# V projected over high and low halves and transposed, VectorE's masks ahead of its decays, halved level sums, one-comparison picks, and the last norm ahead of the branch

## The reference, cut to what matters

```
x    = LN(x)
proj = x @ w_in                       # q, f, v, output gate: 8 heads x 128 each; conv pair; two gates
logf, k = functions of f              # forget gate and key
per head, blocks of 64 tokens:        # gated linear recurrence, 128x128 state S
   b    = cumsum(logf)
   attn[t,s] = sum_d q[t,d] k[s,d] exp(b[t,d] - b[s,d])   for s <= t
   o    = attn @ v + (q exp(b)) @ S ;   S = exp(b_last) S + (k exp(b_last - b))^T @ v
A    = rms_norm(o) * silu(g) @ w_o_a
B    = conv module (31 taps, LayerNorm, silu) @ w_o_b
x    = LN(alpha x + (sig(gate_a) A + sig(gate_b) B) @ w_out)
router: 16 experts, best of 4 groups, then top 2 in it
x    = LN(alpha x + sum_e gate_e * (silu(x Wg_e) * (x Wu_e)) Wd_e)
```

## Time and profile before

| | us |
|---|---|
| median of 3 runs | 913.27 (912.89 to 913.73) |
| the profiled execution | 911.96 |
| its span | 910.1 |
| TensorE busy | 848.2 (93%) |
| VectorE busy | 397.4 (44%) |
| ScalarE busy | 227.5 (25%) |
| GpSimd busy | 108.1 (12%) |
| mean granted TensorE clock | 0.989 |

### The profile page before, as it was taken

One profiled execution on the slowest core, in us unless ns is written; L12 is line 12 of the kernel. 1 busy time (PEld: TensorE's weight loads), 2 busy tenths in 40 slices (PEclk: granted clock), 3 DMA queues, 4 the chain that ended last, 5 costly groups with the idle time before them and its releaser, 6 DMA issues.

```text
span 910.1 us, 12810 instructions
## 1 busy us (share of the span) xinstructions
PE 848.2 (93%) x4904; PEld 532.4 (58%) x4904; DVE 397.4 (44%) x720; ACT 227.5 (25%) x358; POOL 108.1 (12%) x173
## 2 busy tenths in 40 slices
PE   4999999999999999999999999999999899898983
PEld 3989888898989866546554353535435244252330
DVE  6787788879999823215310313103031040310205
ACT  6566666653356131003010011000100001000001
POOL 1366667620000000000000000000000000000000
PEclk9999999999999999998999999999999999999997
DMA  8222222524436523905499999999999999999951
GB/s 302 71 79 80 78 78 85 188 80 154 171 104 237 212 107 153 372 0 208 163 429 428 428 428 428 426 428 427 429 427 429 428 428 428 428 428 428 427 255 59
DMA packets 30420, 248.95 MB, mean 274 GB/s; under 512 B 4462, under 2 KB 7918, under 8 KB 17962
## 3 DMA queue, kind: packets, MB, share of 16 engines
q1 hardware_dynamic: 27840, 247.07, 66.2%
q10 hardware_dynamic: 2538, 1.32, 0.5%
HBM read 245.89 MB, written 2.48 MB: 273 GB/s over the span
## 4 chain that ended last, share of the span: by engine, by line
PE 53%; DVE 19%; DMA 15%; POOL 5%; issue 4%; ACT 3%; POOLq 0%; DVEq 0%; ACTq 0%; SPq 0%
PE ps L437 52%; DMA ring<-in_w_up_e 8%; DMA ring<-in_w_gate_e 7%; DVE ar L1503 6%; DVE split_t L1511 3%; POOL ring L1240 2%; DVE ring L1390 1%; DVE ring L1403 1%; POOL ring L1226 1%; PE ps L772 1%; DVE split_w L1349 1%; POOL ar L1255 0%; DVE mid L1521 0%; POOL ar L1253 0%; DVE split_w L1354 0%
## 5 line engine op out<-in xcount | busy, mean ns | idle before, releaser
L437 PE MATMUL ps<-ring,ar 128*64 128x512 f32 (+1 forms) x1120 | 268.2, 594 | 10.6 <-DMA ring<-in_w_gate_e 3.9
L437 PEld LDWEIGHTS ps<-ring,ar 128*64 128x64 f32 (+1 forms) x1120 | 99.1, 140 | 168.5 <-issue 152.6
L437 PE MATMUL ps<-ring,xT 128*64 128x512 f32 (+2 forms) x896 | 161.4, 458 | 7.0 <-DMA ring<-in_w_gate_e 6.7
L437 PEld LDWEIGHTS ps<-ring,xT 128*64 128x64 f32 (+1 forms) x896 | 84.3, 152 | 79.0 <-issue 63.8
L1720 DVE TENSOR_TENSOR ar<-ar,ps 128x512 f32<-128x512 f32 (+1 forms) x42 | 28.7, 684 | 224.4 <-PE ps L437 224.4
L437 PE MATMUL ps<-split_x,split_t 128*128 128x320 f32 x672 | 101.7, 313 | 4.7 <-DVE split_t L1511 4.1
L437 PEld LDWEIGHTS ps<-split_x,split_t 128*128 128x128 f32 x672 | 100.1, 191 | 6.0 <-issue 3.8
L437 PE MATMUL ps<-split_x,split_w 128*128 128x320 f32 x480 | 80.4, 324 | 6.6 <-DVE split_w L1354 2.7
L437 PEld LDWEIGHTS ps<-split_x,split_w 128*128 128x128 f32 x480 | 73.8, 195 | 11.1 <-issue 2.5
L437 PE MATMUL ps<-ar 128*64 128x64 f32 (+6 forms) x304 | 74.1, 375 | 3.1 <-ACT ar L1174 1.2
L1503 DVE SCALAR_TENSOR_TENSOR ar<-ar,params 128x350 f32<-128x350 f32 x116 | 67.7, 584 | 4.1
(11 more groups left out here) (190 smaller groups left out, 721.8 us busy)
## 6 DMA issues: line engine op xcount, KB each, us to landing
ring<-in_w_gate_e SPq DMA_DIRECT2D x32, 2048.0 KB, 27.5
ring<-in_w_up_e SPq DMA_DIRECT2D x32, 2048.0 KB, 25.9
ring<-in_w_down_e SPq DMA_DIRECT2D x32, 2048.0 KB, 31.7
ring<-in_w_in SPq DMA_DIRECT2D x56, 512.0 KB, 4.3
ring<-in_w_o_a SPq DMA_DIRECT2D x8, 512.0 KB, 5.9
ring<-in_w_out SPq DMA_DIRECT2D x1, 4096.0 KB, 14.6
ring<-in_w_o_b SPq DMA_DIRECT2D x4, 512.0 KB, 5.1
ar<-in_x_prompt SPq DMA_DIRECT2D x2, 512.0 KB, 4.5
```

The source lines that it names most:

```text
L437: return pe.matmul(out, lhsT, rhs, start=start, stop=stop)
```

## The change

Five groups of edits.

1. V goes through `project` as F and Q do, with features on the partitions. ScalarE makes a third high piece (`w_high(..., 2)`), VectorE a third low piece (`w_low(..., 2)`). ScalarE copies the product out of PSUM into a new buffer `hvT` (`v_features`), TensorE transposes it in three pieces (`v_tokens`, behind `prev_out`), and ScalarE's `v_copy` takes it from there.
2. VectorE does both masks before `level_decay`, and a new addition `level_fold` (three banks of 192 columns) takes over GpSimd's two first additions. GpSimd is left with three. The copy into `hebl` moves from VectorE to ScalarE.
3. The position table holds slot + 1, zero where a token isn't chosen. A pair's picks are one copy and one comparison over 384 columns, its gate picks one multiplication.
4. x1's first tile is transposed before the last mix tile; two `keep_busy` calls before the logits go, eight become six and two become one. `gather` signals each half, and `gate` waits for the second half only at its third group.
5. The last norm is applied tile by tile between the statistics, ahead of the branch; in the branch it would be done again.

```diff
+            def v_tokens(i, b):
+                pe.wait_ge(h["vT_sb"], 2 * i + b + 1)
+                for t, (t0, n) in enumerate(TILES):
+                    last = pe.transpose(ps[0:n, 3, t * P:t * P + P], hvT[:, t0:t0 + n], ident)
+                last.then_inc(h["vt_done"], 1)
...
             def cur_v(i, b, first):
-                value_tile(b, 0)
-                value_tile(b, 1)
-                value_tile(b, 2).then_inc(h["v_done"], 1)
+                n = 2 * i + b
+                pe.wait_ge(wlo_ready, 3 * n + 3)
+                if not first:
+                    pe.wait_ge(h["v_sb"], n)
+                project(3, piece(wh, 2), piece(wl, 2)).then_inc(h["v_done"], 1)
...
                 cur_v(*cur, first)
                 if prev:
                     prev_out(*prev, first_prev)
+                v_tokens(*cur)
```

ScalarE, in `head_turn` and in what it calls:

```diff
+            def v_features(i, b):
+                n = 2 * i + b
+                act.wait_ge(h["v_done"], n + 1)
+                signal(act, act.activation(hvT, ps[:, 3, 0:T], ACT.Copy), h["vT_sb"], n + 1)
...
             def v_copy(i, b, first):
-                act.wait_ge(h["v_done"], n + 1)
+                act.wait_ge(h["vt_done"], n + 1)
...
                 cc(act.activation(heb, hb, ACT.Exp))
+                cc(act.activation(hebl[:, b, :], heb[:, SEQ - 1:T:DEC], ACT.Copy))
...
                     u_high(1)
                 elif not first:
                     w_high(*nxt, 1)
+                v_features(*cur)
+                if nxt:
+                    w_high(*nxt, 2)
                 v_copy(*cur, first)
```

VectorE and GpSimd:

```diff
+            def level_fold(i, b):
+                n = 2 * i + b
+                signal(dve, dve.tensor_tensor(hAM[:, :, 0:3 * BLK], hAM[:, :, 0:3 * BLK], hAM[:, :, 4 * BLK:LW], ALU.add), h["fold_ready"], n + 1)
...
                 forget_in(*cur, first or first_prev)
-                level_decay(*cur)
                 if prev:
                     level_mask(*prev, first_prev)
                     last_mask(*prev, first_prev)
+                    level_fold(*prev)
+                level_decay(*cur)
...
                 carry_side(*cur, first)
+                if nxt:
+                    w_low(*nxt, 2)
...
-                pc(pool.tensor_tensor(am[:, :, 0:3 * BLK], am[:, :, 0:3 * BLK], am[:, :, 4 * BLK:LW], ALU.add))
...
+                pool.wait_ge(h["fold_ready"], n + 1)
+                pc(pool.tensor_tensor(hAM[:, :, 0:2 * BLK], hAM[:, :, 0:2 * BLK], hAM[:, :, 2 * BLK:4 * BLK], ALU.add))
+                signal(pool, pool.tensor_tensor(hAS[BLK:P, 0:2, BLK:P], hAM[BLK:P, 0:2, 0:BLK], hAM[BLK:P, 0:2, BLK:2 * BLK], ALU.add), h["as_ready"], 2 * n + 1)
+                signal(pool, pool.tensor_tensor(hAS[0:BLK, :, 0:BLK], hAM[0:BLK, :, 0:BLK], hAM[0:BLK, :, BLK:2 * BLK], ALU.add), h["as_ready"], 2 * n + 2)
```

Router, picks and end:

```diff
                 last.then_inc(mix_done, 1)
+                if t == 1:
+                    to_features(x1, x1_ready, x1T_done, x1T_sb, X1_BANKS, 0, 1)
...
-            to_features(x1, x1_ready, x1T_done, x1T_sb, X1_BANKS, 0, 2)
-            keep_busy(2)
+            to_features(x1, x1_ready, x1T_done, x1T_sb, X1_BANKS, 1, 2)
             logits(0)
+            logits(1)
             to_features(x1, x1_ready, x1T_done, x1T_sb, X1_BANKS, 2, 3)
-            logits(1)
             logits(2)
-            keep_busy(8)
+            keep_busy(6)
...
+                signal(dve, dve.tensor_tensor(pm4, slots_wide, slot_of(cur[:, 0]), ALU.is_equal), e["pick_ready"], n + 1)
...
+            scattered(0)
+            stats2(0, 128, step, 0)
+            gain2(0, 128, step)
+            scattered(1)
+            stats2(1, 128, step, 0)
+            offset2(0, 128)
+            gain2(1, 128, step)
+            scattered(2)
+            stats2(2, 64, step, 0)
+            offset2(1, 128)
+            gain2(2, 64, step)
+            offset2(2, 64)
             more = dve.value_load(flag[0:1, :], min_val=0, max_val=1)
```

More of the change, by code:

```diff
@@ L729, in _ @@
             last.then_inc(pos_done, 1)
-            keep_busy(2)
+            keep_busy(1)
             def both(bank, lhs, g):
@@ L869, in _, with rstd_of @@
             act.wait_ge(setup_done, 1)
-            def rstd_of(var, ready, ch, t):
-                act.wait_ge(var, t + 1)
+            def rstd_of(var, ready, ch, t, before=0):
+                act.wait_ge(var, before + t + 1)
                 ch(act.activation(rstd3[:, t:t + 1], mv[:, t, 1:2], ACT.Ln, bias=eps1[:, :]))
-                signal(act, act.activation(rstd3[:, t:t + 1], rstd3[:, t:t + 1], ACT.Exp, scale=-0.5), ready, t + 1)
+                signal(act, act.activation(rstd3[:, t:t + 1], rstd3[:, t:t + 1], ACT.Exp, scale=-0.5), ready, before + t + 1)
             def copy_features(dst, done, copied, banks):
@@ L933, in _ @@
                     signal(act, act.activation(xT[:, k, :], ps[:, k, 0:T], ACT.Identity, scale=g_in[:, k:k + 1], bias=b_in[:, k:k + 1]), xh_ready, XT_A[k])
+            w_high(0, 0, 2, True)
             act.wait_ge(params_ready, 1)
@@ L1196, in _ @@
             expert_pair(PAIRS // 2 - 1, 1, end=True)
+            act.preload_act_table_set("natural_log_exp_and_others")
+            for t in range(3):
+                rstd_of(var2, rstd2, step, t)
             more = act.value_load(flag[0:1, :], min_val=0, max_val=1)
             with act.If(more != 0):
+                act.preload_act_table_set("silu_and_others")
                 with act.Fori(1, ROUNDS) as r:
@@ L1202, in _ @@
                         late_pair(PAIRS // 2 * r + i, 1)
-                act.wait_ge(var2, 6)
-            act.preload_act_table_set("natural_log_exp_and_others")
-            for t in range(3):
-                rstd_of(var2, rstd2, step, t)
+                act.preload_act_table_set("natural_log_exp_and_others")
+                for t in range(3):
+                    rstd_of(var2, rstd2, step, t, 3)
         @block.gpsimd
@@ L1297, in norm_stats, with norm_gain, norm_offset @@
                     ch(dve.bn_stats(stats[0:n, t, hf, :], halves[hf]))
-            def norm_apply(dst, src, t, n, g, b, rstd, ready, ch):
+            def norm_gain(dst, src, t, n, g, ch):
                 ch(dve.scalar_tensor_tensor(dst, src, mv[0:n, t, 0:1], g, ALU.subtract, ALU.mult))
-                dve.wait_ge(rstd, t + 1)
-                signal(dve, dve.scalar_tensor_tensor(dst, dst, rstd3[0:n, t:t + 1], b, ALU.mult, ALU.add), ready, t + 1)
+            def norm_offset(dst, t, n, b, rstd, ready, before=0):
+                dve.wait_ge(rstd, before + t + 1)
+                signal(dve, dve.scalar_tensor_tensor(dst, dst, rstd3[0:n, t:t + 1], b, ALU.mult, ALU.add), ready, before + t + 1)
             def stats0(t, n, halves):
@@ L1358, in _ @@
             w_low(0, 0, 1)
+            w_low(0, 0, 2)
             dve.wait_ge(mask_in, 16)
@@ L1412, in carry_side @@
                 dve.wait_ge(h["k_ready"], n + 1)
-                cc(dve.tensor_copy(hebl[:, b, :], heb[:, SEQ - 1:T:DEC]))
                 if not first:
```

116 lines of the change are left out of this document (48 added, 68 removed).

## The result

The changed kernel takes 953.51 us (median of 4 runs, 953.31 to 954.46); the kernel before took 913.08 us beside it (911.71 to 913.73). The ratio is 1.0448 [1.0436, 1.0461], 40.4 us slower. The forecast was 953.

A forecast was written before the change was run, and what follows sets the result against it. It took head turns to be full on TensorE, with a GpSimd chain as long. 911.96 + 27.7 (ring) + 16 (clock) - 1.0 (router) - 1.75 (end) = 952.9; with the median 1.3 above the profiled execution, forecast 953 us, range 931 to 970.

The forecast's parts named there:

- The ring: Head turns: a loop of waits through TensorE, ScalarE and VectorE, closed by V's copy, adds 27.7 us.
- The clock: Head turns: TensorE's granted clock falls after each of eight new pauses, 2.0 us each, 16 us in all.
- 4.1 + 2.9 + 13.6 + 2.9: Head turns: added us for turn 0, turn 1, the four looped turns together, and turn 6.
- two events: TensorE's earlier slow stretches: 1.6 us lost after a 2.17 us pause, some 3 us after the start's idle time.
- TensorE's one pause in front of the transposes: Head turns: TensorE idles some 4 to 5 us per turn before V's new transposes, released by ScalarE's copy.
- VectorE as next bound: Rival, head turns: VectorE's 20.1 us per turn sets the pace, about 909 to 912 us; chance 0.06.
- V's saving worth nothing: Head turns: the 1.3 us per turn saved on TensorE gain nothing, since it then waits until 119.6.
- Router, -1.0: Router up to the first gate: reordering, fewer keep_busy and shorter picks together give about -1.0 us, bounds -3 and +3.
- End, -1.75: Kernel's end: 1.55 us ahead of the first gain go and gains fill scatter waits, -1.75 us, bounds -3 and 0.
- the clock holds: Rival, head turns: the loop of waits is right but TensorE's pauses cost nothing, 937 us; chance 0.22.
- TensorE stays the bound: Rival, head turns: V's copy ends before prev_out does, turns shrink by 1.65 us, 897 us; chance 0.05.
- Half clock for all restarted work: Rival, head turns: all work restarted after a pause runs at half clock, 4.3 us per pause, 971 us; chance 0.15.

The follow-up runs named there:

- e2: The changed kernel with 28 unused matmuls ahead of prev_out and 12 ahead of V's transposes, filling TensorE's waits; 940.99 us, ratio 1.0321.
- e6: The changed kernel with ScalarE's q_copy and prev_cross ahead of level_exp instead of behind it; 943.94 us, ratio 1.0344.
- e3: The changed kernel with V's transposes behind the next forget projection and v_copy behind the next forget; 944.01 us, ratio 1.0347.
- e5: The changed kernel with V in full float32 again, without copy, transposes or third weight pieces; 926.95 us, ratio 1.0165.
- e8: The changed kernel with V's transposes and v_copy late, and q_copy and prev_cross ahead of level_exp; 924.36 us, ratio 1.0134.
- e12: e10 with 18 unused matmuls ahead of prev_out, in TensorE's wait for GpSimd's sums; 916.26 us, ratio 1.0037.
- e10: The changed kernel with decays ahead of masks, V's transposes behind the next forget projection, and the router's old order of transposes and keep_busy; 927.98 us, ratio 1.0172.
- e13: e10 with V in full float32 at its old place; 912.84 us, ratio 0.9997.
- e1: The kernel before with only edit groups 3 to 5 (picks, router order, last norm), head turns untouched; 913.05 us, ratio 0.9995.
- e9: The kernel before with only one-comparison picks, split gather signals and the early last norm, old router order kept; 910.12 us, ratio 0.9976.
- e11: e3 with 24 unused matmuls ahead of prev_out, in TensorE's wait for prev_cross; 934.87 us, ratio 1.022.

## Why the prediction was right, step by step

- **The ring, 27.7 us: right, for more reasons than I gave.** From VectorE's start (99.20) to the end of V's copy (115.51) are 16.31 us in turn 4, where the prediction has 16.15 (103.40 to 119.55). Inside it errors cancel: up to the end of the fold 5.40 instead of 5.70, since the fold follows the mask without a wait; the decays with their gap 4.22 instead of 3.55, since they take 4.19 and not 3.40; from there to the copy's end 6.69 instead of 6.90. With the clock held (e2), a turn is 23.6 where the sum said 23.5, and from turn 0's start to the first tap e2 takes 30.0 us more than the kernel before, 1.6 of them in the slow work behind the pause that it leaves: 28.4 for the ring. That V's copy closes the ring is shown by e6, where prev_out no longer waits for ScalarE, the transposes still wait for V's copy, and turns are still 23.9. Taking V's copy out alone (e3) is not enough, since `prev_cross` closes a ring nearly as long.
- **The clock, 16 us: right in size, in part by luck.** From turn 0's start to the first tap e2 gives back 14.0 for the seven pauses that it fills, 2.0 each, and the eighth costs 1.6. In turn 4, from the end of V's copy (115.51) to `forget` (122.37) are 6.86 us, where the prediction has 4.55 at full clock: 2.3 for the pause, in one of the long turns. At the start of turn 7 the shift is 37.4; the prediction's terms up to there give 4.1 + 2.9 + 13.6 + 2.9 and seven pauses of 2.0, 37.5. Here turns 0 and 1 cancel: turn 0 grew by 5.1 where the terms say 6.1, turn 1 by 6.1 where they say 4.9. The 2.0 was a choice between two events. At the second, the start, the row shows a granted clock of 1.00, and only the count of matmuls speaks for a low one. e5 has the same 9 matmuls from 22 to 24 at 0.50, so the reading holds.
- **TensorE's one pause in front of the transposes: wrong in its place.** I had prev_out done long before V's copy. It waits itself for `prev_cross`, which the prediction lists as a link that the late `level_exp` delays, without asking who else waits for it. The pause is two, 25.9 and 17.7 us in all. The sum hardly changes, as only the second lies on the ring; but e3's expectation, drawn from this picture, missed by 14 us.
- **VectorE as next bound: mis-sized.** The prediction has its list at 20.1 us. e8 shows it all but full at 21.1, the decays' 0.8 being most of the difference, and a ring of ScalarE and VectorE as long. The prediction moved the decays and kept their 3.40 without asking what GpSimd does beside them at the new place. With the decays first (e12) turns are 20.3.
- **V's saving worth nothing: right, and too mild.** e10, e12 and e13 put V's new form at 15 us even where its copy holds up nothing (928.0 against 912.8), 12 of them by the clock.
- **Router, -1.0: half.** From the first tap to the first gate -0.5. The last mix tile came 0.9 later, as worked out, and the picks took 0.56. The new pause ahead of the logits, which the prediction names as a bound only, came, and the low clock behind it with it. e1 against e9 puts the whole new order at 2.9 us in the medians, but at 1.7 by the ratios to the kernel before beside each, and their intervals overlap.
- **End, -1.75: right.** -1.7 between the last scatter and the end of the span.

The rivals: at e2's 941 one has nearly the time for "the clock holds" (937), so that case was worked out rightly and simply did not occur; the unfilled pause (1.6) and the slow gather (1.6) are most of the rest. For the case that TensorE stays the bound, the prediction puts the mark at 111 in turn 4. By its own numbers V ends at 113.3 and prev_out at 114.7, which is the mark; the copy at 119.55 misses this one too, so nothing hangs on it. Half clock for all restarted work was too much: the forget projection took 5.06 to 6.17, and twice 3.78 would be 7.56.

Open: which of the two engines holds up the other where the decays meet GpSimd's sums. The meetings are seen in every turn, and are gone with the other order, but no run moves one of the two instructions alone. Open as well is why e1 and e9 have two groups of times, and why the clock falls in the logits without a pause.

## What to carry to other kernels

A wait in the middle of an in-order list delays all that is written behind it: before moving one, go round the loop engine by engine until it closes, and then list everybody else who waits for each delayed link. Where TensorE is full and others are nearly so, a cheaper matmul is worth nothing until they are faster, and may cost time, where the wait that it opens lowers the clock for the work behind it. To tell a clock loss from a dependency, fill the pause with matmuls that nobody reads: what comes back is the clock, unless another engine takes over as the bound (e11). And when work moves to another place in an engine's list, look at what the other engines do there: the decays cost 3.40 at one place and 4.19 at the other.

## What the runs showed of the hardware

- Waits of 1.2 to 2.0 us, one per turn, left the granted clock at 1.00 (e5, 60 to 160 us). One of 2.3 to 2.4 per turn went with 0.87 (e10), two of together 5.4 (43.6 in eight turns) with 0.83 (the changed kernel). The length alone didn't decide: behind a wait of 2.21 in e5 the forget projection took 5.32, behind one of 2.23 in e2 (turn 0) the next 48 matmuls took 7.28, which is full speed.
- The low clock can begin some time after the pause. In turn 1 of e10 prev_out ran at full speed right behind a wait of 3.09 (granted clock 1.00 from 57.0 to 58.4), and the projection behind it was slow (0.50 from 58.8 to 62.0; 5.32 instead of 3.78):

```profile
57.06 1.44 PE L438 MATMUL ps<-ar 128*128 128x128 f32 x10 [3.09 <-POOL ar L1276]
```

- Nor does it end with the first matmuls: in the changed kernel prev_out took 2.56 (1.44 in e5), transposes 0.90 instead of 0.55, and of the 24 matmuls behind them a part still ran slow; the projections after those were at full speed again (48 in 7.31).
- Matmuls of 16 columns suffer too: the 32 of the logits took 7.01 in e1 (granted clock 0.50 from 418 to 422), and 4.11 in the kernel before (0.69). There the clock fell with no pause ahead: TensorE was busy 3.93 and 4.00 of 4 us.
- A VectorE subtraction begun 0.13 behind a GpSimd sum of 1.02 took 1.06 (the changed kernel). Beside GpSimd's pieces of 0.45 to 0.51 the seven took 0.29 to 0.50 each (the kernel before).
- 24 unused matmuls of 192 columns took 2.83 us, 0.118 each.
